# Feature-major x and memory, split first products and a shorter root chain in a two-layer decoder trunk

## What is computed

```python
h = rms_norm(x, norm_mix[l])
qkv = (h @ w_in[l]).reshape(B, S, 3, 16, 64)      # 1024 x 3072 weights
...                                               # q, k: rms norm per head, rotary on a quarter of the features
o_a = diff_attention(...)                         # 4 heads, softmax(s1) - lam * softmax(s2)
o_b = dilated_mixture(qb, kb, vb)                 # 6 heads
o_c = moba_attention(qc, kc, vc)                  # 6 heads
x = x + concat(o_a, o_b, o_c) @ w_out[l]
x = x + memory_cross_attention(rms_norm(x), rms_norm(mem), ...)   # 4 heads, k and v from mem @ w_mkv
x = x + (silu(g) * u) @ w_down[l]                 # g, u = rms_norm(x) @ w_gate_up, D_FF 2816
```

## Time and profile before

| what | value |
|---|---|
| median of 3 runs | 686.60 us (686.38 to 686.66) |
| profiled execution, span from first to last instruction | 684.7 us |
| TensorE, weight loads | 99%, 82% busy |
| VectorE, ScalarE, GpSimd | 73%, 58%, 15% busy |
| DMA | 115.65 MB, mean 169 GB/s |

### The profile page before, as it was taken

One profiled execution on the slowest core, in us unless ns is written; L12 is line 12 of the kernel. 1 busy time (PEld: TensorE's weight loads), 2 busy tenths in 40 slices (PEclk: granted clock), 3 DMA queues, 4 the chain that ended last, 5 costly groups with the idle time before them and its releaser, 6 DMA issues.

```text
span 684.7 us, 10697 instructions
## 1 busy us (share of the span) xinstructions
PE 676.3 (99%) x3746; PEld 563.6 (82%) x3746; DVE 499.6 (73%) x960; ACT 394.1 (58%) x647; POOL 105.8 (15%) x127
## 2 busy tenths in 40 slices
PE   8999999999999999999999999999999999999997
PEld 7787777878888888888888878778788888888886
DVE  5799977587766666666678798875877666666665
ACT  6977776477544444444566669664865444444442
POOL 5254020236000000000034230202620000000000
PEclk9999999999999999999999999999999999999999
DMA  9945542146666666666547535214366666666631
GB/s 322 324 147 185 166 143 62 62 124 184 185 184 184 184 184 188 186 196 196 193 146 247 192 115 185 93 58 119 101 186 207 194 190 195 193 186 184 184 122 62
DMA packets 121392, 115.65 MB, mean 169 GB/s; under 512 B 2704, under 2 KB 95376, under 8 KB 121360
## 3 DMA queue, kind: packets, MB, share of 16 engines
q1 hardware_dynamic: 120784, 114.31, 53.8%
q10 hardware_dynamic: 576, 0.93, 0.4%
HBM read 114.17 MB, written 1.05 MB: 168 GB/s over the span
## 4 chain that ended last, share of the span: by engine, by line
PE 88%; DVE 5%; ACT 4%; DMA 1%; issue 1%; SPq 0%; POOL 0%; DVEq 0%; POOLq 0%; ACTq 0%
PE ps L1975 22%; PE ps L1582 19%; PE ps L1982 12%; PE ps L2023 6%; PE ps L2024 6%; PE ps L2025 6%; PE ps L1653 3%; DVE wlo L952 2%; PE ps L2004 2%; PE ps L1735 2%; PE ps L1908 2%; PE ps L1714 2%; PE ps L1771 1%; PE ps L1502 1%; DMA raw<-in_w_in 1%
## 5 line engine op out<-in xcount | busy, mean ns | idle before, releaser
L952 DVE TENSOR_TENSOR wlo<-raw,whi 128x2048 fp32r<-128x2048 f32 (+1 forms) x95 | 212.0, 2249 | 45.5 <-ACT whi L637 43.2
L637 ACT ACTIVATE whi<-raw 128x2048 fp32r<-128x2048 f32 (+1 forms) x102 | 188.5, 1875 | 11.7 <-PE ps L2025 6.5
L1975 PE MATMUL ps<-both,whi 128*128 128x512 f32 x672 | 167.2, 391 | 0.0
L1975 PEld LDWEIGHTS ps<-both,whi 128*128 128x128 f32 x672 | 123.4, 188 | 23.8
L1582 PE MATMUL ps<-whi,both 128*128 128x512 f32 x384 | 99.6, 395 | 1.8 <-ACT qkv L697 0.9
L1982 PEld LDWEIGHTS ps<-both,wlo 128*128 128x128 f32 x672 | 91.7, 190 | 6.5
L1982 PE MATMUL ps<-both,wlo 128*128 128x256 f32 x672 | 94.1, 283 | 0.0
L890 ACT ACTIVATE qkv<-ps 128x512 f32<-128x512 f32 x42 | 25.1, 598 | 112.7 <-PE ps L1982 112.7
L1582 PEld LDWEIGHTS ps<-whi,both 128*128 128x128 f32 x384 | 70.5, 188 | 17.7 <-ACT qkv L697 1.5
L2023 PE MATMUL ps<-whi,ahi 128*128 128x512 f32 x176 | 69.3, 394 | 0.0
L2024 PE MATMUL ps<-wlo,ahi 128*128 128x512 f32 x176 | 69.0, 392 | 0.0
(11 more groups left out here) (213 smaller groups left out, 873.9 us busy)
## 6 DMA issues: line engine op xcount, KB each, us to landing
raw<-in_w_gate_up SPq DMA_DIRECT2D x88, 512.0 KB, 5.0
raw<-in_w_in SPq DMA_DIRECT2D x23, 1024.0 KB, 5.5
raw<-in_w_down SPq DMA_DIRECT2D x22, 1024.0 KB, 5.0
raw<-in_w_out SPq DMA_DIRECT2D x8, 1024.0 KB, 5.0
raw<-in_w_mkv SPq DMA_DIRECT2D x4, 1024.0 KB, 5.2
raw<-in_w_mq SPq DMA_DIRECT2D x4, 512.0 KB, 3.5
raw<-in_w_mo SPq DMA_DIRECT2D x2, 1024.0 KB, 4.8
xs<-in_x SPq DMA_DIRECT2D x4, 256.0 KB, 5.5
```

The lines of the kernel that those rows point to most:

```text
L637: ins = act.activation(whi[s][:, cols], raw[s][:, cols], ACT.Copy)
L952: ins = dve.tensor_tensor(wlo[s][:, cols], raw[s][:, cols], hi, ALU.subtract)
L1975: pe.matmul(ps[:, bank, :], whi[s][:, a:a + P], both[:, :, k, :], start=(k == 0), stop=False)
```

## The change

- x and memory also come feature-major (`x_columns`, `mem_columns`), laid out ahead on the host. The first chunk of x features rides on the first load of ScalarE's queue (`first_load`), the others come on SP between the first eight weight pieces. TensorE transposes neither x of layer 0 nor memory. The row tiles of x come later, for the squares; memory by rows comes after unit 11, once all its low parts are made, into the same buffer.
- The first chunk is computed feature chunk by feature chunk (`first_products`), with splits of 256 columns of x and 512 columns of weights. Units 2 and 3 are split and waited for in halves (`split_half`).
- Six accumulators (FIRST_BANKS) are used before one is used again.
- The angles' last steps run on VectorE (`reduce_angles`). ScalarE's first activation is a sine, so the first table is that of the sine.
- The root chain has one step less in its second round (`inverse_root`), and the factor is in the scale of the squares.
- In layer 0 the memory parts, the squares and the root of memory and lambda are at other fillers. `T_AT` of the second head is 57 for both layers. `lambda_products` and `root` have other places on GpSimd.

```diff
-                        if layer == u == 0:
-
-                            for k in range(4):
-                                sp.dma_start(view(0, 4)[:, k, :], w_in[:, k, 512 * c:512 * c + 512]).then_inc(s_first[k].sem, 16)
-                            for q in FIRST_ORDER[1:]:
-                                x_quarter(q)
+                        cols = slice(512 * c, 512 * c + 512)
+                        if layer == 0 and u < 2:
+
+                            for k in range(4 * u, 4 * u + 4):
+                                sp.dma_start(view(u, 4)[:, k % 4, :], w_in[:, k, cols]).then_inc(s_first[k].sem, 16)
+                                for n, (at, chunks) in enumerate(X_COLUMN_LOADS):
+                                    if k == at:
+                                        x_columns(n, chunks)
                             continue
-                        load(layer, u, [(view(u, 4), w_in[:, 4 * h:4 * h + 4, 512 * c:512 * c + 512])])
-                        if layer == 0 and u == RING:
+                        if layer == 0 and u < 4:
+                            if u == 3:
+                                for t in range(T):
+                                    sp.dma_start(xs[:, t, :], x_in[:, t, :]).then_inc(s_x[t].sem, 16)
+                                sp.wait_ge(hi_done[0].sem, 1)
+                                sp.wait_ge(lo_done[0].sem, 1)
+                            for half in range(2):
+                                k = 4 * h + 2 * half
+                                sp.dma_start(view(u, 4)[:, 2 * half:2 * half + 2, :], w_in[:, k:k + 2, cols])\
+                                  .then_inc(s_halves[u - 2][half].sem, 16)
+                            continue
+                        load(layer, u, [(view(u, 4), w_in[:, 4 * h:4 * h + 4, cols])])
+                        if layer == 0 and u == MEM_COLUMNS_AFTER:
+                            sp.dma_start(mem_sb[:].rearrange("p t d -> p (t d)"), consts["mem_columns"]).then_inc(s_memT.sem, 16)
+                        if layer == 0 and u == MEM_AFTER:
+
+                            sp.wait_ge(m_lo.sem, 4)
                             sp.dma_start(mem_sb[:], mem.rearrange("b (t p) d -> p (b t) d", p=P)).then_inc(s_mem.sem, 16)
...
-                link(pool.tensor_scalar(turns, turns, -magic, None, ALU.add))
...
-                for n in range(len(TWO_PI)):
-                    link(pool.tensor_tensor(flat, flat, two_pi[n], ALU.add))
-                link(pool.tensor_scalar(ang[:, 0], ang[:, 0], math.pi / 2, None, ALU.add))
-                pool.tensor_scalar(ang, ang, 3.1415925, -3.1415925, ALU.min, ALU.max).then_inc(s_cs.sem, 1)
+                pool.tensor_scalar(turns, turns, -magic, None, ALU.add).then_inc(s_turns.sem, 1)
...
-            act.dma_start(starter[:], consts["starter"]).then_inc(s_starter.sem, 16)
+            act.dma_start(first_load[:], consts["starter"]).then_inc(s_starter.sem, 16)
             act.wait_ge(s_ones.sem, 1)
-            act.activation(copy_warm[:], ones[:, 0:8], ACT.Copy)
+            act.activation(copy_warm[:], ones[:, 0:8], ACT.Sin)
...
+            def first_x(k):
+
+                if k == 0:
+                    act.wait_ge(s_starter.sem, 16)
+                for n, (_, chunks) in enumerate(X_COLUMN_LOADS):
+                    if k == chunks[0]:
+                        act.wait_ge(s_xcols[n].sem, 16)
+                act.activation(thi[:, k, :], x_cols[k], ACT.Copy, scale=g_rows[:, 0, G_MIX, k:k + 1]).then_inc(first_x_hi.sem, 1)
...
+                if q == 0:
+                    act.wait_ge(s_memT.sem, 16)
+                act.activation(two_chunks(mhi, q), two_chunks(mem_cols, q), ACT.Copy).then_inc(m_hi.sem, 1)
...
+                    for k in range(KC):
+                        first_x(k)
+                        if k:
+                            first_weights(k)
+                    act.dma_start(ident_turn[:], consts["ident_turn"]).then_inc(s_rot.sem, 16)
                     act.dma_start(small[:].rearrange("p l n -> p (l n)"),
                                   gains["small"].to_broadcast((P, DEPTH * N_SMALL))).then_inc(s_small.sem, 16)
                 else:
                     for q in range(2 * T):
                         x_hi(layer, X_MIX, q)
-                for t in range(T):
-                    squares_of_x(layer, 0, t)
+                    for t in range(T):
+                        squares_of_x(layer, 0, t)
                 split_hi(layer, 2)
+                if layer == 0:
+                    for t in range(T):
+                        squares_of_x(layer, 0, t)
+                    split_half(3, 0)
...
-                    if layer == 0 and g == 9:
+                    if layer == 0 and g == SIN_AT:
 
                         act.wait_ge(s_cs.sem, 1)
                         act.activation(cs[:], ang, ACT.Sin).then_inc(s_sin.sem, 1)
...
                     if layer == 0 and g == MEM_SQ_AT:
 
                         act.wait_ge(s_mem.sem, 16)
-                        act.wait_ge(ss_done.sem, 1)
                         for t in range(T):
-                            ins = act.activation(sq[:, t * D:(t + 1) * D], mem_sb[:, t, :], ACT.Square,
+                            ins = act.activation(mem_sb[:, t, :], mem_sb[:, t, :], ACT.Square,
                                                  accum_out=mem_ss[:, t:t + 1])
                         ins.then_inc(s_memss.sem, 1)
-                    if layer == 0 and g == LAM_AT + 3:
+                    if layer == 0 and g == LAM_EXP_AT:
                         act.wait_ge(s_lam.sem, 1)
                         act.activation(lam_exp[:], lam_dot[:], ACT.Exp).then_inc(s_lam.sem, 1)
...
+            def inverse_root(n, sign, out=None):
 
 
                 v, y, t, u = (a[:, 0:n] for a in (nv, ny, nt, nh))
-                link(dve.tensor_scalar(y.bitcast(I32), v.bitcast(I32), -0.5, 1597463007.0 - (sign < 0) * 2.0 ** 31,
+                link(dve.tensor_scalar(y.bitcast(I32), v.bitcast(I32), -0.5, 1597463007.0 - (sign > 0) * 2.0 ** 31,
                                        ALU.mult, ALU.add))
-                for c in (1.0, ROOT_STEP):
-                    link(dve.tensor_tensor(t, y, v, ALU.mult))
-                    link(dve.tensor_tensor(t, t, y, ALU.mult))
-                    link(dve.scalar_tensor_tensor(u, t, -10.0 / 3.0 * c, t, ALU.add, ALU.mult))
-                    if c == 1.0 or out is None:
-                        link(dve.scalar_tensor_tensor(y, u, 5.0 * c * c, y, ALU.add, ALU.mult))
-                    else:
-                        link(dve.scalar_tensor_tensor(out, u.rearrange("p (t g) -> p t g", t=T), 5.0 * c * c,
-                                                      y.rearrange("p (t g) -> p t g", t=T), ALU.add, ALU.mult))
+                link(dve.tensor_tensor(t, y, v, ALU.mult))
+                link(dve.tensor_tensor(t, t, y, ALU.mult))
+                link(dve.scalar_tensor_tensor(u, t, -10.0 / 3.0, t, ALU.add, ALU.mult))
+                link(dve.scalar_tensor_tensor(y, u, 5.0, y, ALU.add, ALU.mult))
+                link(dve.tensor_tensor(t, y, v, ALU.mult))
+                link(dve.tensor_tensor(t, t, y, ALU.mult))
+                if out is None:
+                    link(dve.scalar_tensor_tensor(y, t, -64.0 / 3.0, y, ALU.add, ALU.mult))
+                else:
+                    link(dve.scalar_tensor_tensor(out, t.rearrange("p (t g) -> p t g", t=T), -64.0 / 3.0,
+                                                  y.rearrange("p (t g) -> p t g", t=T), ALU.add, ALU.mult))
...
+            def reduce_angles():
+
+                dve.wait_ge(s_turns.sem, 1)
+                flat, whole = (a.rearrange("p i t f -> p (i t f)") for a in (ang, turns))
+                for part in TWO_PI:
+                    link(dve.scalar_tensor_tensor(flat, whole, -part, flat, ALU.mult, ALU.add))
+                link(dve.tensor_scalar(ang[:, 0], ang[:, 0], math.pi / 2, None, ALU.add))
+                dve.tensor_scalar(ang, ang, 3.1415925, -3.1415925, ALU.min, ALU.max).then_inc(s_cs.sem, 1)
...
+                    dve.wait_ge(s_first[0].sem, 16)
+                    dve.tensor_copy(whi[0][:, 0:512], raw[0][:, 0:512]).then_inc(first_hi_dve.sem, 1)
+                    for k in range(KC):
+                        first_x(k)
+                        first_weights(k)
+                    reduce_angles()
                 else:
                     for q in range(2, 4):
                         x_lo(layer, X_MIX, q)
-                ask_roots_of_x(layer, 0)
+                    ask_roots_of_x(layer, 0)
                 split_lo(layer, 2)
+                if layer == 0:
+                    ask_roots_of_x(layer, 0)
                 take_roots_of_x(layer, 0)
+                if layer == 0:
+                    for half in range(2):
+                        cols = slice(1024 * half, 1024 * half + 1024)
+                        if half:
+                            dve.wait_ge(hi_done[0].sem, 2)
+                        else:
```

(62 more changed lines are left out.)

303 lines of the change are left out of this document (145 added, 158 removed).

## The result

The changed kernel takes 693.4 us (median of 4 runs, 690.47 to 694.61) against 686.6: 1.0094 times as long, 95% interval 1.0080 to 1.0109. It is slower by 6.8 us. I had said slower, but 689.3, and 693.4 is outside my range of 684.2 to 691.3. One further execution of the kernel before took 1352.4 us, about twice the others, and is left out of its median. The profiled execution of the changed kernel has a span of 692.4 us, 7.7 more than before.

What follows compares the result with a forecast made beforehand. TensorE, busy 676.3 of 684.7 us, bounds the kernel; the question was whether VectorE and ScalarE follow its earlier start. First probabilities +1.3, memory squares +2.1, layer 1 -0.7 give +2.7: 689.3 us, range 684.2 to 691.3.

Steps and rivals of the forecast that it cites:

- TensorE's own work, and the start: First 40 us: 32 transposes (3.6 us) go, products begin at 5.2, first chunk ends at 16.8; TensorE alone 5.4 us early.
- Can the keys follow: First keys in layer 0: ready at 37.4, TensorE waits there and is from then on 3.0 us early, not 5.4.
- My alternative for the small tables: Loads at the start: all small tables go ahead of x's second tile; G is 2.4 and the end 0.6 us later.
- The stretch to the first probabilities: Layer 0: last memory part stands behind a weight split, TensorE waits 4 us and starts the next stretch 1.3 us late.
- My formula, combined at 68.4-G: First probabilities: VectorE has its last memory part, reciprocal, factor and product done at 68.4 us less G.
- rival 4: Start: after the shorter warm-up eight products at 1.2 GHz lose 1.6 us, end moves by 0 to 0.5, 689.6; chance 0.08.
- Squares of memory: ScalarE, ahead of the copies of the keys: all 2.1 us counted as loss, lower bound 0.
- Layer 1: Second transposition of probabilities comes 12 products later instead of 4, so the 0.68 us wait at 402.56 goes: -0.7.
- Faster: Rival 2: keys in time, ready at 35, G 5.4, memory squares cost nothing; 684.8, deciding from G above about 5; chance 0.20.

## Why the prediction was wrong in size

By its own steps:

- **TensorE's own work, and the start: right.** First products at 5.10 (5.2 forecast), first chunk done at 16.5 (16.8). The first accumulator was moved out at 20.8 (21.3), with some luck: the second tile's square began at 17.5 where I had 18.6, but from there it took 3.3 us and not 2.7, because the split of half of unit 3, whose load ScalarE waited for, stood in front. TensorE reached the keys at 37.0, with 1.4 us of waits for splits in it: 35.6 without, against 35.3 (5.4 us early).
- **"Can the keys follow": the step that failed.** G is how much earlier than before TensorE gets on at the first keys. I had G = 3.0 us early; it was 0.3 late. Behind the first accumulator, which was even ahead of the forecast, I carried over the chain of the kernel before with small corrections. I left out that the split of unit 4 stands ahead of the keys' root and can't move forward with the squares, because its load comes no earlier (1.4 us more idle time), and that VectorE, rid of the memory parts, comes to a second split while the rotation is open (1.9 us more). Moving the root, or the second split, took 3 us off the time each (690.1 and 690.4), so both are shown. That x's row tiles, besides the small table, hold up unit 4 is only argued: no run moved them. My alternative for the small tables was beside the point. It drew on the Trainium skill, "DMA: Bandwidth & Descriptors", section "Queues, rings and completion order", by which a DMA engine takes turns between the queues that have work. From this I had worked out that the small tables would hold up x's second tile. Without the larger of them that tile's square began no earlier (17.76 against 17.50); what came earlier was the load behind the tile. How the engines took their turns no run here shows.
- **The stretch to the first probabilities: right in mechanism.** VectorE idle, last memory part behind the split, a wait of 3.3 us for a forecast 4. Taking the parts away removed the wait. My formula, combined at 68.4-G, gives 68.7 with the true G; it was done at 70.1, since the slow clock behind the keys held up the third chunk, on whose squares VectorE waited.
- **The clock: the term that was missing.** I had weighed a slow clock only at the start (rival 4). I forecast two standstills, of 2.4 and 4 us, and gave them only their own length. The one behind the keys cost 2.1 us more, the one behind the probabilities nothing, because other engines were as late.
- **Squares of memory: too large.** 2.1 us in the sum, 1.3 in the stretch (15.23 to 13.97) and 1.0 between the medians. The same stretch keeps 1.1 us over the kernel before after they have moved; where that goes, beside waits of 0.56 and 0.24 us for VectorE, no run took apart. (The stretch ahead of it is 0.5 shorter than before.)
- **Layer 1: wrong.** -0.7 in the sum; the change of place alone gave nothing. From second queries to the end the changed kernel is 0.4 us shorter, for which the shorter root chains are an untested candidate.

Put together: with the keys 3.3 us later than in the sum and 2.1 of slow clock, 2.7 becomes 8.1, less 0.8 for the squares, plus 0.3 for layer 1, 7.6, where the two spans differ by 7.7. So close a match is partly luck: the same sum puts the first probabilities at 70.8, where they came at 70.3, and the stretch behind them 0.6 us too short. The rival of a slow start came true in part: in 5 of the 12 profiled executions with WARM 7 the first six products took 2.9 us instead of 1.75 to 2.2. The gap behind the warm-up was 0.6 to 0.9 us and not 1.1. How far it moved the end no run isolates: these five executions lie from 3.0 us below to 2.0 above the medians of their kernels, and the longer warm-up gained nothing by itself. In its three profiles the six took 2.3, 2.4 and 1.7 us. "Faster" failed where I had put its condition, G above 5. It failed by order: nearly the same work with one table and some steps moved is 2.8 us faster than the kernel before (683.9), and with two more warm-up multiplications and the later split of unit 6 3.6 us (683.0).

## What to carry to other kernels

When an engine is freed ahead of a chain that crosses several others, work out again for each link what it now meets, above all loads that come no earlier, or are pushed back by added data, and steps in fixed orders that wait for them, and don't carry over the old distances. A forecast standstill of TensorE of several microseconds is to be priced with slow products behind it, and then checked against what the other engines could have delivered there anyway. Before giving up a change that removes work but loses time, look for the two or three instructions that stand in front of what TensorE waits for: here a few numbers in the tables of places, one moved load and a slightly longer warm-up turned +6.8 us into -3.6.
